# Attention products with the values stationary in two column tiles, issued in three parts per block, and constant products taken out

## What is computed

```python
s = jnp.einsum('bqgrd,bqkgd->bqgrk', qg, ksel).astype(jnp.float32) * attn_scale + bias
s = jnp.where(valid[:, :, None, None, :], s, -jnp.inf)
p = jax.nn.softmax(s, axis=-1).astype(vsel.dtype)
o = jnp.einsum('bqgrk,bqkgd->bqgrd', p, vsel)
...
y_attn = attn @ w_branch_attn[layer]
```

## Time and profile before

| | |
|---|---|
| runs | 1744.24, 1747.75, 1750.28 us; median 1747.75 |
| profiled execution | 1747.64 us, of which the span of the profile is 1745.8 |
| PE, busy share of the span | 93% |
| DVE | 59% |
| ACT | 41% |
| POOL | 29% |
| beginning, to the end of the last `ada_cols` | 0 to 60 us |
| attention, rounds 0 to 31 | 662 to 807 us |
| first branch product | 819 us |

### The profile page before, as it was taken

How to read it: one execution, slowest core, us unless ns; L and a number is a source line. 1 busy time by engine, 2 the same in 40 slices (tenths; PEclk the granted TensorE clock), 3 DMA queues, 4 the chain that set the end, 5 groups by cost and what they waited for, 6 DMA issues and landing times.

```text
span 1745.8 us, 21984 instructions
## 1 busy us (share of the span) xinstructions
PE 1617.3 (93%) x7923; PEld 1311.7 (75%) x7923; DVE 1033.2 (59%) x1678; ACT 710.5 (41%) x1130; POOL 511.3 (29%) x379
## 2 busy tenths in 40 slices
PE   5997899999999998998998956999999999998996
PEld 4683477888888886887887845788888888887875
DVE  4677999835647487654444486665555555335345
ACT  5225523154666566565012333433334333222232
POOL 1310012233535332232002055445544543002001
PEclk9998999999999999998999978999999999999998
DMA  9562211221211223001433411222322222843441
GB/s 328 171 252 60 73 37 49 82 88 49 67 53 53 83 85 121 2 2 61 145 148 142 133 49 48 73 79 92 97 72 72 83 85 97 311 145 109 145 174 67
DMA packets 133807, 177.96 MB, mean 102 GB/s; under 512 B 9438, under 2 KB 91481, under 8 KB 133724
## 3 DMA queue, kind: packets, MB, share of 16 engines
q1 hardware_dynamic: 125082, 157.98, 27.8%
q10 hardware_dynamic: 8066, 16.78, 2.5%
q0 software_dynamic: 576, 2.10, 0.3%
HBM read 143.79 MB, written 32.52 MB: 101 GB/s over the span
## 4 chain that ended last, share of the span: by engine, by line
PE 84%; DVE 7%; ACT 3%; issue 3%; POOL 1%; DMA 1%; SPq 0%; DVEq 0%; ACTq 0%; POOLq 0%
PE pp L519 23%; PE pp L520 23%; PE pp L521 23%; PE pp L1474 6%; PE pp L1480 3%; PE pp L1666 3%; PE pp L1775 2%; DVE arena L2034 2%; DVE cb_lo L2381 1%; DVE h_part L2356 1%; DVE h_raw L2004 0%; ACT arena L1139 0%; PE pp L1502 0%; PE pp L1656 0%; DMA arena<-in_x 0%
## 5 line engine op out<-in xcount | busy, mean ns | idle before, releaser
L519 PE MATMUL pp<-cb_hi,wp_hi 128*128 128x512 f32 x616 | 243.8, 396 | 27.7 <-DVE cb_lo L2381 14.6
L520 PE MATMUL pp<-cb_lo,wp_hi 128*128 128x512 f32 x616 | 242.6, 394 | 0.0
L521 PE MATMUL pp<-cb_hi,wp_lo 128*128 128x512 f32 x616 | 242.3, 393 | 0.0
L937 POOL TENSOR_TENSOR wp_sum<-raw 128x512 f32<-128x512 f32 x110 | 147.5, 1349 | 241.7 <-PE pp L521 240.1
L2365 DVE TENSOR_TENSOR wp_lo<-wp_sum,wp_hi 128x512 fp32r<-128x512 f32 x110 | 94.1, 857 | 160.3 <-ACT wp_hi L1365 160.1
L832 POOL TENSOR_TENSOR e_lo<-arena,e_hi 128x1024 fp32r<-128x1024 f32 (+1 forms) x38 | 95.3, 2509 | 299.0 <-ACT e_hi L1024 299.0
L519 PE MATMUL pp<-hT_hi,e_hi 128*128 128x512 f32 x416 | 167.6, 403 | 4.2 <-DVE hT_lo L1989 1.8
L2056 DVE TENSOR_SCALAR_CACHE_REDUCE arena<-arena,bound 128x384 bf16<-128x384 f32 (+2 forms) x192 | 169.4, 941 | 0.8
L521 PE MATMUL pp<-hT_hi,e_lo 128*128 128x512 f32 x416 | 163.6, 393 | 0.0
L520 PE MATMUL pp<-hT_lo,e_hi 128*128 128x512 f32 x416 | 163.5, 393 | 0.0
L519 PEld LDWEIGHTS pp<-cb_hi,wp_hi 128*128 128x128 f32 x616 | 117.6, 191 | 54.2 <-issue 29.7
(11 more groups left out here) (254 smaller groups left out, 3272.3 us busy)
## 6 DMA issues: line engine op xcount, KB each, us to landing
arena<-in_w_ada SPq DMA_DIRECT2D x48, 512.0 KB, 7.9
raw<-in_w_ffn_down SPq DMA_DIRECT2D x44, 512.0 KB, 3.5
arena<-in_w_in SPq DMA_DIRECT2D x33, 512.0 KB, 3.9
raw<-in_w_ffn_gate SPq DMA_DIRECT2D x22, 512.0 KB, 4.6
raw<-in_w_ffn_up SPq DMA_DIRECT2D x22, 512.0 KB, 5.0
hidden_t<-stage SPq DMA_DIRECT2D x22, 512.0 KB, 3.1
hid_in<-hidden_t SPq DMA_DIRECT2D x44, 256.0 KB, 3.7
gates_t<-arena ACTq DMA_DIRECT2D x32, 256.0 KB, 2.1
```

Of the source, the lines that this page charges most:

```text
L519: nc.tensor.matmul(out, ah, bh, start=start and k == 0, stop=False)
L520: nc.tensor.matmul(out, ah, bl, start=False, stop=False)
L521: last = nc.tensor.matmul(out, al, bh, start=False, stop=stop and k == len(pairs) - 1)
L937: pool.tensor_tensor(wp_sum[n % 4], ff_weight(m, a), ff_weight(m, b), op).then_inc(sum_ready, 1)
```

## The change

1. `weigh` now works on a whole block at once. The values of a group (64 channels) are stationary, in the column tile that the group's number gives, and the turned weights of the group's four heads move, 512 columns at a time. The two groups write the two halves of the partitions of one bank, for each key tile one product a group. The result has channels in the partitions and queries in the columns.
2. The products of a block are issued in three parts, in rounds 1, 2 and 3 of the next block, after that round's scores and ahead of its transposes.
3. `pT` holds whole blocks: three places for the turned weights of a group in the wide blocks (`pT_at`), one of which is the place of the branch weights, whose loads therefore wait for the third block's product (`pv_full`, 3).
4. The row sums are spread: DVE writes 1/sum for 64 channels a head (`attn_scale`), PE turns that with four products (`rinv_turned`), ACT copies it to SBUF (`rinv_copy`), DVE multiplies (`attn_norm`). `attn_out` on PE is gone; ACT and DVE make the rounded parts from SBUF.
5. A branch weight tile of the attention is loaded in two transfers of 64 partitions, in the new order of the heads; three transfers a tile where there were two.
6. All `keep_busy` products are out, and `pick` is made earlier, so that its semaphore goes.

```diff
-    pT = [at(C0 + 1024 * i, NT, P) for i in range(4)]
+    pT_at = [C0, G0, H0, C0, G0, H0, C0, G0, G0 + 8192, G0 + 11776, C0, C0 + 2048, G0, G0 + 2048, E0 + 1024, E0 + 1536]
...
+    def pT_heads(b, g):
+        return at(pT_at[2 * (NT - 1 - b) + g], 4, P * (b + 1))
...
-        sp.wait_ge(bias_full, 4)
+        sp.wait_ge(pv_full, 3)
...
-            for r in range(2):
-                sp.dma_start(raw[:, m % 4, 4 * P * r:4 * P * (r + 1)].rearrange("p (k c) -> p k c", c=P),
-                             wbr[r][:, :, m * P:(m + 1) * P]).then_inc(raw_full[m % 4], 16)
+            for g in range(2):
+                rows = T["w_branch_attn"][0][4 * HD * g:4 * HD * (g + 1), m * P:(m + 1) * P].rearrange("(k p) c -> p k c", p=HD)
+                sp.dma_start(raw[HD * g:HD * (g + 1), m % 4, 0:4 * P].rearrange("p (k c) -> p k c", c=P), rows).then_inc(raw_full[m % 4], 16)
+            sp.dma_start(raw[:, m % 4, 4 * P:8 * P].rearrange("p (k c) -> p k c", c=P), wbr[:, :, m * P:(m + 1) * P]).then_inc(raw_full[m % 4], 16)
...
+        def rinv_copy(b):
+
+            act.wait_ge(rows_full, b + 1)
+            if b:
+                act.wait_ge(o_read, b)
+            act.activation(rinv_rows, bank[(b + 1) % 2], ACT.Copy).then_inc(rows_copied, 1)
...
-            if j >= 7 and j % 4 == 3:
-                attn_out(j // 4 - 1)
+            if j >= 6 and j % 4 == 2:
+                rinv_copy(j // 4 - 1)
+            if j >= 8 and j % 4 == 0:
+                attn_out(j // 4 - 2)
...
-        keep_busy(bank[4], 8)
         ada_parts(1)
         ada_cols(1)
...
-        keep_busy(bank[4], 20)
         key_part("kk", 0, range(4))
-        keep_busy(bank[4], 8)
         ada_parts(2)
...
-            whole(bank[turn_of % 2][:, h * HD:(h + 1) * HD],
-                    [(pT[i % 4][:, c, :], v_tok[:, c, (h // 4) * HD:(h // 4 + 1) * HD]) for c in range(b + 1)]).then_inc(pv_full, 1)
...
+        def weigh(x, part):
+
+            b = ORDER[x]
+            n = b + 1
+            if part == 0:
+                pe.wait_ge(pt_free, NH * (x + 1))
+                if b >= 4:
+                    pe.wait_ge(pt_free2, NH * (x + 1))
+                if x:
+                    pe.wait_ge(rows_copied, x)
+            for c in range((n * part + 2) // 3, (n * part + n + 2) // 3):
+                for g in range(2):
+                    last = pe.matmul(bank[x % 2][HD * g:HD * (g + 1), :], v_tok[:, c, HD * g:HD * (g + 1)],
+                                     pT_heads(b, g)[:, :, c * P:(c + 1) * P], start=(c == 0), stop=(c == b))
+                if c == b:
+                    last.then_inc(pv_full, 1)
+
+        def rinv_turned(x):
+
+            pe.wait_ge(wide_ready, x + 1)
+            if x:
+                pe.wait_ge(o_read, x)
+            for k in range(4):
+                last = pe.matmul(bank[(x + 1) % 2][:, k * P:(k + 1) * P], rinv_wide[:, k].rearrange("p g d -> p (g d)"), ident[:, :], start=True, stop=True)
+            last.then_inc(rows_full, 1)
 
         for j in range(PAIRS + 2):
             if j < PAIRS:
                 scores(j)
+            if j >= 5 and j % 4:
+                weigh(j // 4 - 1, j % 4 - 1)
+            if j >= 6 and j % 4 == 2:
+                rinv_turned(j // 4 - 1)
             for e in range(2):
                 if 1 <= j <= PAIRS:
                     turn(2 * (j - 1) + e)
-                if j >= 2:
-                    weigh(2 * (j - 2) + e)
-            if j >= 7 and j % 4 == 3:
-                attn_out(j // 4 - 1)
...
+        def attn_scale(b):
+
+            dve.wait_ge(p_ready, NH * (b + 1))
+            if b:
+                dve.wait_ge(rows_full, b)
+            link(dve.reciprocal(rinv[:, :], rsum[:, NH * (b % 2):NH * (b % 2) + NH]))
+            dve.tensor_copy(rinv_wide, rinv[:, :].rearrange("p (g k) -> p k g", g=2).unsqueeze(3).broadcast_to([P, 4, 2, HD])).then_inc(wide_ready, 1)
...
+            if j >= 4 and j % 4 == 0:
+                attn_scale(j // 4 - 1)
+            if j >= 8 and j % 4 == 0:
+                attn_norm(j // 4 - 2)
+            if j >= 9 and j % 4 == 1:
+                attn_rest(j // 4 - 2)
```

More of the change, by code:

```diff
@@ L241, in build, with pT @@
     rinv = sb("rinv", [P, 8])
+    def pT_heads(b, g):
+        return at(pT_at[2 * (NT - 1 - b) + g], 4, P * (b + 1))
+    def pT(b, h):
+        return pT_heads(b, h // 4)[:, h % 4, :].rearrange("p (c t) -> p c t", t=P)
     far_max = sb("far_max", [P, 2])
@@ L360, in build @@
     o_read = sem("o_read")
-    at_full = sem("at_full")
+    wide_ready = sem("wide_ready")
+    rows_full = sem("rows_full")
+    rows_copied = sem("rows_copied")
     attn_hi_ready = sem("attn_hi_ready")
@@ L705, in _ @@
         gv = gates_d.rearrange("(g m p) t -> p m g t", g=2, p=P)
-        wbr = [T[n][0].rearrange("(k p) c -> p k c", p=P) for n in ("w_branch_attn", "w_branch_rec")]
+        wbr = T["w_branch_rec"][0].rearrange("(k p) c -> p k c", p=P)
         for m in range(KD):
@@ L1295, in unload @@
             b, h = ITEMS[i]
-            if i >= 4:
-                act.wait_ge(pv_full, i - 3)
+            if i >= NH + 4:
+                act.wait_ge(pv_full, (i - 4) // NH)
             n = min(4, b + 1)
             act.wait_ge(pt_full, PT_GROUPS[i] + 1)
-            act.activation(pT[i % 4][:, 0:n, :], bank[6 if i < WIDE else 6 + i % 2][:, 0:n * P].rearrange("p (c t) -> p c t", t=P),
+            act.activation(pT(b, h)[:, 0:n, :], bank[6 if i < WIDE else 6 + i % 2][:, 0:n * P].rearrange("p (c t) -> p c t", t=P),
                            ACT.Copy).then_inc(pt_free, 1)
+        def rinv_copy(b):
[3 more added lines that the diff above has]
+            act.activation(rinv_rows, bank[(b + 1) % 2], ACT.Copy).then_inc(rows_copied, 1)
         def attn_out(b):
-            act.wait_ge(at_full, b + 1)
-            act.activation(attn_hi[:, :, ORDER[b] * P:(ORDER[b] + 1) * P], bank[b % 2].rearrange("p (c t) -> p c t", t=P), ACT.Copy).then_inc(attn_hi_ready, 1)
+            act.wait_ge(o_read, b + 1)
+            act.activation(attn_hi[:, :, ORDER[b] * P:(ORDER[b] + 1) * P], attn_raw.rearrange("p (c t) -> p c t", t=P), ACT.Copy).then_inc(attn_hi_ready, 1)
         for j in range(PAIRS + 1):
@@ L1314, in _ @@
                 rec_root()
-            if j >= 7 and j % 4 == 3:
-                attn_out(j // 4 - 1)
+            if j >= 6 and j % 4 == 2:
+                rinv_copy(j // 4 - 1)
+            if j >= 8 and j % 4 == 0:
+                attn_out(j // 4 - 2)
             if j in (PAIRS - 4, PAIRS - 3):
                 split_hi(act, j - PAIRS + 4)
-        for n in range(2 * RH):
+        for n in range(4):
+            turned_hi(n)
+        rinv_copy(NT - 1)
+        for n in range(4, 2 * RH):
             turned_hi(n)
@@ L1488, in _ @@
         pe.wait_ge(cact_ready, 1)
-        def keep_busy(out, n):
-            for _ in range(n):
-                pe.matmul(out[:, 0:P], ident[:, :], ident[:, :], start=True, stop=True)
         def ada_parts(j):
@@ L1519, in _ @@
         pe.wait_ge(vcol_ready, 1)
-        pe.wait_ge(pick_ready, 1)
         ada_parts(0)
@@ L1719, in bias_turned @@
         def bias_turned(j):
-            pe.wait_ge(flip_ready, 1)
+            pe.wait_ge(ident_ready, 2)
             pe.wait_ge(bias_loaded, 16)
@@ L1820, in _ @@
                     rec_turned(n)
+        rinv_turned(NT - 1)
         for n in range(4, 2 * RH):
             rec_turned(n)
-        attn_out(NT - 1)
         pe.wait_ge(attn_lo_ready, NT)
@@ L1933, in _ @@
         link(dve.memset(vrows[:, :], 1.0))
+        dve.wait_ge(ident_ready, 1)
+        link(dve.tensor_reduce(pick[:, :], ident[:, 0:P:32], AX.X, ALU.add))
         dve.wait_ge(cact_ready, 1)
@@ L2237, in read_scores @@
                                      scalar=start, op0=ALU.add, op1=ALU.min, accum_out=top).then_inc(s_read, 1)
+        def attn_scale(b):
[4 more added lines that the diff above has]
+            dve.tensor_copy(rinv_wide, rinv[:, :].rearrange("p (g k) -> p k g", g=2).unsqueeze(3).broadcast_to([P, 4, 2, HD])).then_inc(wide_ready, 1)
         def attn_norm(b):
-            dve.wait_ge(pv_full, NH * (b + 1))
+            dve.wait_ge(pv_full, b + 1)
+            dve.wait_ge(rows_copied, b + 1)
             if b:
[L2242 to L2245, removed]
+                dve.wait_ge(attn_lo_ready, b)
+            dve.tensor_tensor(attn_raw, bank[b % 2], rinv_rows, ALU.mult).then_inc(o_read, 1)
         def attn_rest(b):
@@ L2276, in _ @@
                         rec_norm(t, h)
+            if j >= 4 and j % 4 == 0:
[4 more added lines that the diff above has]
+                attn_rest(j // 4 - 2)
             if j in (PAIRS - 4, PAIRS - 3):
                 split_lo(dve, j - PAIRS + 4)
[L2279 to L2282, removed]
+        attn_rest(NT - 2)
         for n in range(4):
```

33 lines of the change are left out of this document (10 added, 23 removed).

## The result

The changed kernel takes 1764.16 us (median of 4 runs, 1763.19 to 1768.97), the kernel before 1748.63 (4 runs): a ratio of 1.0097, 95% interval 1.0084 to 1.0111. Forecast was 1741.0, with 1731 to 1751. The profiled execution is the longest of the four.

A forecast was written before the change was run, and what follows sets the result against it. PE, with 84% of the chain, was taken to bound the kernel, with DVE's chain limiting gains in wide rounds. From 1747.64 us, attention -3.4 and constant products -3.4 gave 1740.8, stated as 1741.0; range 1731 to 1751.

The forecast's parts named there:

- The products: Products with the values: tiles overlap, 0.86 us a key tile, 31 us for all 36, half of 62.
- the rival that they don't: Products' tiles overlap less: without any overlap +31 us, 1772; halfway 1756; chance 0.15.
- Rounds 2 and 3, and 4 to 7: Attention's blocks 7 and 6: -2.35 us in rounds 2 and 3, +1.5 in rounds 4 to 7 (28.7 against 27.2).
- I price them at nothing: `attn_scale`, `attn_norm`, `rinv_copy` at a round's end: nothing, DVE's under 1.4 us covered; uncovered, up to 1.4 in seven rounds.
- Rounds 8 to 15: Attention's blocks 5 and 4: 46.2 us against 43.85, so +2.35.
- the wait is not there: Rival: head A's unload comes early enough, wide rounds are PE's, 25 + 39 us for 74.9: 1730; chance 0.12.
- Rounds 16 to 27: 34.8: Attention's blocks 3 to 1: PE's work counts, 34.8 us against 39.4, so -4.6.
- Round 28 on: -0.3: End of the attention: DVE and ACT bound it, only a reciprocal and a wait go, -0.3 us (bounds 0 and -1).
- The constant products: -3.4: Beginning: quarter 1 starts 1.8 us sooner, third call gives 1.9, sum 3.7, less 0.3 for the clock: -3.4.
- My bound of about 0: Removing the beginning's constant products gains about 0 if the clock stayed low through quarters 2 and 3.
- The branch loads, third places for `pT`: Attention: both cost nothing; loads needed some 35 us later; without that cover round 28 late by 5.5 to 7.2 us.
- landed within 7.2, by 33.9: Beginning: quarter 1's data, issued until 26.7, landed within 7.2 us, by 33.9, so quarter 1 starts 1.8 us sooner.

The follow-up runs named there:

- experiment 6: Changed kernel with ACT waiting for `wide_ready` instead of `o_read`, and a block's first two parts between head A's and head B's transposes, row sums behind them: 1743.82 us, 0.9982.
- experiment 1: Changed kernel with one ACT wait changed: a block's first exponentials wait for `wide_ready` (row sums read) instead of `o_read` (block normed): 1752.45 us, ratio 1.0016.
- experiment 7: The kernel of experiment 6 with all 36 constant products of the beginning put back: 1745.03 us, ratio 0.9975.
- experiments 1 to 6: Experiment 1, experiment 6, and between them: filler before part 0 (1774.85 us), beginning's constants back (1766.38), kernel before without them (1746.18), changed kernel with DVE's norm earlier (1751.87).

## Why the prediction was wrong

By its own steps:

- **The products.** Right. A part of three tiles took 2.73 us from its start to the transposes (690.28 to 693.01), forecast 2.8. The tiles overlap; the rival that they don't, the only one I had for a clearly slower kernel, had nothing in it. Its figure from the Trainium skill (TensorE: Matmul & The Clock Gate, Part 3), 2.38 times for three column tiles, does not carry over to this shape: two column tiles here have twelve records of 0.427 us, as the prediction has one of 512 columns, in 2.73, so 1.88 times, near the full two. No run here has three tiles.
- **Rounds 2 and 3, and 4 to 7.** Right: 22.81 us for rounds 0 to 3 against 23.0, 28.09 against 28.7. The part's delay of head A's unload is there, and experiment 6 shows that it is the place that costs.
- **`attn_scale` and `attn_norm`: "I price them at nothing".** This is the step that failed. I looked at who queues behind them on DVE, and found cover of 1.27 to 1.35 us up to the next reading; that holds: in experiment 1, DVE's reading after the norm of round 8 starts at 718.68 us, 0.1 behind the scores. In the changed kernel the same reading starts 1.3 us late, held up by ACT's exponentials and not by DVE's own work. I did not ask who waits for their signal. The norm moves from the end of round 4n - 2 to the end of round 4n, its signal with it, and ACT's exponentials in round 4n wait for it. Cost: 12.2 us of waits and 5.4 of clock, where the forecast had nothing; none of my rivals was this. The code shows it without any trace: one signal that changes its place, and one line that waits for it, which the diff doesn't touch.
- **Rounds 8 to 15.** With that wait gone 45.03 us, forecast 46.2: 1.2 to the good. The rival "the wait is not there" had 64 us for rounds 4 to 15, and experiment 6, which moved the parts, took 67.84: it was false of this order of the code, and most of it could be had by another.
- **Rounds 16 to 27: 34.8.** Wrong by 3.3 even without the wait (38.10 in experiment 1). I counted PE's work there and took it that PE never waits. In rounds 16, 20 and 24, which have no part, it waits 2.1 us in all for ACT's unloads and exponentials, and PE idles 2.95 us of the 40 from 758 to 798. Before, the products of a head stood between the transposes of A and B, and in the same stretch PE had no gap. The other 1.2 I didn't trace.
- **Round 28 on: -0.3.** Wrong: +1.5 in experiment 1. Rounds 28 to 30 are 1.0 longer there (7.93 for 6.94), now with parts and row sums in them; which of these does it was not tried.
- **The constant products: -3.4.** Right in one of two courses of the beginning, and nothing in the other (last section). My bound of about 0 had the clock low through quarters 2 and 3; they ran at the full clock (32 records in 3.64 us), and it was quarter 1 that came late and at half.
- **The branch loads, third places for `pT`.** Priced at nothing, and no wait of PE, ACT or DVE in the attention of the changed kernel's trace names either. The loads are the traffic of 760 to 780 us (98 GB/s, rows above) and done by then; round 28 begins at 811. Neither was tried alone.

The differences of the table, sorted by these steps: attention forecast 153.8, plus 17.6 for the wait in its six rounds and 0.7 net in the rounds beside them (1.3 more in round 26, where the clock was low, and 0.7 less from 28 on), 3.3 for rounds 16 to 27, 1.8 for the end, less 1.2 for rounds 8 to 15, 0.6 for 4 to 7 and 0.2 for 0 to 3, makes 175.2; measured 175.22. That is 18.0 over before, and with the start 2.2 sooner 15.8. As the terms are differences of measured rounds they must close; what experiments bear out is the 17.6.

So the change does take work from PE: from 655 to 832 us the products with the values are busy for 35.5 us in experiment 1 and for 72.0 before, and the products of the row sums take 9.3 of that back. In the wide rounds DVE's chain takes most of it, as forecast; the leftover wait turned the rest into a loss. Cured, with the parts between the heads, the kernel is 0.2% faster than before, and 0.35 to 0.43% in the three versions that have the ten constant products too.

## What to carry to other kernels

When an edit moves an instruction, list who waits for its semaphore, the lines that the diff does not touch before all, and ask of each what it really needs; a wait that names a neighbour's signal for a buffer's sake keeps its old price only while the neighbour stays where it was. Taking work from an engine also takes the cover from every wait that stood behind that work, and work that must go in somewhere belongs between two steps of which the second waits for another engine, not ahead of both. And a filler is to be costed from its records before it is run.

## What the runs showed of the hardware that was not expected

**The beginning takes one of two courses**, whatever the kernel. PE's 22 transposes from about 23.4 us take 6.5 to 6.8 us or 5.0 (granted clock from 20 to 28 us 0.79 before, 1.00 in the changed kernel); the first ada group then starts at 29.7 to 30.4 or at 28.2 to 28.8. The first key product of `ki` starts, by profile:

| us | constants in | first call only | out |
|---|---|---|---|
| late course | 59.89, 59.15 | 57.71 | 56.13, 56.06, 56.03, 55.80 |
| early course | 58.51 | | 58.41, 58.50, 59.20, 59.21 |

In the late course leaving them out gives 3.5 us, as forecast. In the early one it gives nothing, though only one profile has it with the constants in: there PE waits for the second group's load and then runs all or most of the group at half the clock, where the constants kept it at the full one. Of the changed kernel, PE's timeline:

```profile
34.55 3.64 PE L1520 MATMUL pp<-arena,c_wide 128*32 128x512 f32 x16 [2.68 <-DMA arena<-in_w_ada]
38.90 1.86 PE L1527 MATMUL pp<-pick,arena 128*128 128x1 f32 x8 [0.71 <-ACT arena L1068]
45.39 0.76 PE L528 MATMUL pp<-hT_hi,e_hi 128*128 128x512 f32 x1 [4.62 <-POOL hT_lo L834]
```

and of experiment 6:

```profile
33.59 1.92 PE L1520 MATMUL pp<-arena,c_wide 128*32 128x512 f32 x16
36.23 1.05 PE L1527 MATMUL pp<-pick,arena 128*128 128x1 f32 x8 [0.72 <-ACT arena L1068]
42.21 0.76 PE L528 MATMUL pp<-hT_hi,e_hi 128*128 128x512 f32 x1 [4.92 <-POOL hT_lo L834]
```

My step "landed within 7.2, by 33.9" holds in the second of these, the late course, alone. Without the first call the load landed at 34.55 to 34.9 us in each of the early profiles; in the late ones it was there when PE came for it, at 33.5 to 33.7. The cause stays open.

**One wait, two clocks.** The second scores of the attention stand behind a wait of 3.15 us. In the kernel before, in the changed one and in experiment 7 they ran at the full clock (1.99 us); in experiments 1 to 6 mostly at half (3.42 to 3.79), as here in the first:

```profile
664.89 3.42 PE L1789 MATMUL pp<-arena 64*128 64x512 f32 x8 [3.15 <-DVE nmax L2260]
```

So one profile with a full clock behind a wait is no proof that the next has it. A difference without a changed line is seen after the attention too: from the first branch product to the end the profiles have from 925.0 to 932.6 us, 926.55 before and 932.15 of the changed kernel. These 5.6 us are why the two profiled spans differ by 21.4 us and not by 15.8. Whether the change makes the longer course more frequent stays open: both profiles with the old attention have the short one (under 927 us), and of the ten with the new attention four.
